# The recurrence of a hybrid decoder trunk: the inverse as two chains of two head pairs, and the order of a tick written anew

## What is computed

```python
def step(S, inp):
    r_t, d_t, kk_t, a_t, k_t, v_t = inp
    sa = jnp.einsum('bhvk,bhk->bhv', S, -kk_t)
    S = S * d_t[:, :, None, :] + sa[..., None] * (kk_t * a_t)[:, :, None, :] + v_t[..., None] * k_t[:, :, None, :]
    return S, jnp.einsum('bhvk,bhk->bhv', S, r_t)
...
y = jnp.moveaxis(ys, 0, 1)
mean = jnp.mean(y, axis=-1, keepdims=True)
var = jnp.mean(jnp.square(y - mean), axis=-1, keepdims=True)
y = (y - mean) * lax.rsqrt(var + GN_EPS) * lp['lnx_w'].reshape(N_HEADS_RWKV, HEAD_DIM) + lp['lnx_b'].reshape(N_HEADS_RWKV, HEAD_DIM)
y = y + jnp.sum(r_h * k_h * lp['r_k'], axis=-1, keepdims=True) * v_h
y = y.reshape(B, T, D_RWKV) * g
```

## Time and profile before

| | us |
|---|---|
| median of 3 runs (lowest to highest) | 2150.49 (2148.86 to 2151.88) |
| the profiled execution's own time | 2147.41 |
| its span, first to last instruction | 2145.8 |
| TensorE busy in the span | 2037.6 (95%) |
| VectorE, ScalarE, GpSimd busy | 1200.0 (56%), 622.0 (29%), 163.4 (8%) |

### The profile page before, as it was taken

The page is one execution under the profiler, slowest core; times in us unless marked ns, Lnnn a source line. Parts: engine busy times, 40 slices in busy tenths (PEclk is TensorE's granted clock), DMA queues, the critical chain, the costliest instruction groups (busy, mean ns, idle before and its releaser), DMA issues.

```text
span 2145.8 us, 37700 instructions
## 1 busy us (share of the span) xinstructions
PE 2037.6 (95%) x15476; PEld 1131.8 (53%) x15476; DVE 1200.0 (56%) x2401; ACT 622.0 (29%) x1401; POOL 163.4 (8%) x280
## 2 busy tenths in 40 slices
PE   8999999888888898999988999999999999999999
PEld 6445656788776774444444444444444444444443
DVE  4375654477775448776565445545453636363625
ACT  5005552222322226766644122111111111102020
POOL 3000000222221002222112000000000000000000
PEclk9999999999998997999999999999999999999999
DMA  7001113101013711000054601111111111111102
GB/s 220 0 0 30 30 30 112 43 4 24 4 34 104 194 51 55 11 6 11 1 172 145 201 1 40 39 40 39 40 40 40 39 40 39 39 40 41 43 35 84
DMA packets 96906, 115.77 MB, mean 54 GB/s; under 512 B 32252, under 2 KB 68029, under 8 KB 96671
## 3 DMA queue, kind: packets, MB, share of 16 engines
q1 hardware_dynamic: 90718, 101.82, 15.0%
q10 hardware_dynamic: 4480, 7.34, 1.2%
q0 software_dynamic: 1536, 4.20, 0.6%
HBM read 104.75 MB, written 12.64 MB: 55 GB/s over the span
## 4 chain that ended last, share of the span: by engine, by line
PE 83%; DVE 10%; ACT 4%; issue 2%; DMA 1%; ACTq 0%; POOL 0%; POOLq 0%; DVEq 0%
PE psum L1416 77%; PE psum L1951 2%; PE psum L1835 1%; ACT arena L1286 1%; PE psum L2008 1%; ACT arena L1272 1%; DVE arena L2467 1%; DVE arena L2643 1%; DVE arena L2617 1%; DVE arena L2510 1%; DVE arena L2494 1%; PE psum L1753 0%; PE psum L1501 0%; DVE arena L2457 0%; DVE arena L2506 0%
## 5 line engine op out<-in xcount | busy, mean ns | idle before, releaser
L1416 PE MATMUL psum<-arena 64*64 64x64 f32 (+13 forms) x12520 | 1794.8, 345 | 69.0 <-ACT arena L1286 20.1
L1416 PEld LDWEIGHTS psum<-arena 64*64 64x64 f32 (+5 forms) x12520 | 910.8, 150 | 845.4 <-issue 664.0
L2800 DVE TENSOR_TENSOR arena<-arena,psum 128x512 f32<-128x512 f32 x51 | 35.1, 688 | 318.5 <-PE psum L1416 318.5
L1389 ACT ACTIVATE arena<-psum 128x512 f32<-128x512 f32 x51 | 30.3, 595 | 437.3 <-PE psum L1416 344.7
L1378 ACT ACTIVATE arena<-arena 128x512 f32<-128x512 f32 x64 | 40.2, 628 | 274.2 <-DVE arena L2814 168.0
L938 POOL TENSOR_TENSOR arena<-arena,m_lev 128x256 f32<-128x256 f32 x82 | 59.7, 729 | 552.0 <-DVE arena L2448 362.7
L1272 ACT ACTIVATE arena<-psum 128x512 f32<-128x512 f32 (+1 forms) x148 | 80.7, 596 | 68.9 <-PE psum L1951 60.2
L2617 DVE TENSOR_REDUCE arena<-psum 128x1 f32<-128x640 f32 (+7 forms) x128 | 84.6, 703 | 14.8 <-PE psum L1416 13.2
L1286 ACT ACTIVATE arena<-psum,arena 128x640 f32<-128x640 f32 (+7 forms) x128 | 89.0, 704 | 10.7 <-DVE arena L2617 10.6
L1951 PEld LDWEIGHTS psum<-ident,arena 128*128 128x128 f32 x528 | 58.0, 143 | 46.1 <-issue 22.9
L2467 DVE TENSOR_TENSOR arena<-arena,psum 128x512 f32<-128x512 f32 x65 | 44.5, 684 | 62.8 <-PE psum L1416 62.8
(11 more groups left out here) (324 smaller groups left out, 1808.6 us busy)
## 6 DMA issues: line engine op xcount, KB each, us to landing
arena<-in_w_up_dram SPq DMA_DIRECT2D x7, 2048.0 KB, 7.6
arena<-in_w_down_dram SPq DMA_DIRECT2D x7, 2048.0 KB, 7.7
arena<-in_cache_slc_kv_dram SPq DMA_DIRECT2D x96, 128.0 KB, 2.7
arena<-in_cache_cmp_kv_dram SPq DMA_DIRECT2D x72, 128.0 KB, 3.3
arena<-in_x_prompt_dram SPq DMA_DIRECT2D x16, 512.0 KB, 12.8
arena<-in_cache_cmp_kv_dram ACTq DMA_DIRECT2D x56, 128.0 KB, 3.4
arena<-in_w_in_dram SPq DMA_DIRECT2D x13, 512.0 KB, 3.8
arena<-in_w_in_dram SPq DMA_DIRECT2D x2, 2048.0 KB, 19.6
```

The costliest lines, as they stand in the source:

```text
L1416: return nc.tensor.matmul(out, lhsT, rhs, start=start, stop=stop)
L2800: tt(u2, t_sb, bank_of(6), ALU.add).then_inc(sem("u_sum"), 1)
```

## The change

The inverse of a chunk becomes two chains, one for head pairs 0 and 1 and one for 2 and 3. Each has X, T and U in banks of its own, its copies and subtractions are half as wide, and its steps have semaphore counts of their own. The slots are gone: each engine's tick is one written list, and what isn't the chain stands between the chain's steps. Further: adding the identity (128x512) and the bonus rows (two operations of 128x256) go from VectorE to GpSimd; -u goes from VectorE to ScalarE; the centring takes one operation instead of two; the values are turned between the products of w; the weight (lnw) moves a tick later, to stand before the group norm's end; so does the reciprocal root on ScalarE; the products of the two masks are split (atrb early in bank 0, gtrk at the end in bank 7). The core of the diff (rests of the same kind left out):

```diff
-        inv_step = psum[:, 3 * 512 + 256:4 * 512 + 256]
-        inv_u, inv_t, inv_x = inv_step[:, 0:256], inv_step[:, 256:512], banks[4][:, 256:512]
+        inv_step = [psum[:, 512 * b + 384:512 * b + 640] for b in (3, 1)]
+        inv_u, inv_t = [v[:, 0:P] for v in inv_step], [v[:, P:2 * P] for v in inv_step]
+        inv_x = [banks[b][:, 256:384] for b in (4, 2)]
...
+            def bonus_rows(c):
+                if c == 0:
+                    pool.wait_ge(*once("bonus_out"))
+                else:
+                    pool.wait_ge(sem("rw_yo"), c)
+                link(nc.gpsimd.tensor_tensor(bv, vtok_r[c % 3], spread(bonus[:, c, :], 2, HD), ALU.mult))
+                nc.gpsimd.tensor_tensor(bv, bv, lnb, ALU.add).then_inc(sem("rw_bv"), 1)
...
             for c in range(NCH + 1):
+                pool.wait_ge(sem("rw_ab_sb"), 2 * c + 2)
+                turned = tu_r[c % 3].rearrange("p a b c d -> p (a b c) d")
+                nc.gpsimd.tensor_tensor(turned, turned, spread(eye2, 1, 2 * HP), ALU.add).then_inc(sem("rw_ti"), 1)
                 pool.wait_ge(sem("rw_prod_sb"), 2 * c + 1)
...
+                for i in range(min(nlev(c), 4)):
+                    level_mask(c, i)
+                if c >= 1:
+                    pool.wait_ge(sem("rw_vgsb"), c)
+                    bonus_rows(c - 1)
+                if nlev(c) == 5:
+                    level_mask(c, 4)
...
+            def l_act(c, i, half):
+                if i < nlev(c):
+                    act.wait_ge(sem("rw_x"), 2 * (lev0(c) + i) + half + 1)
+                    nc.scalar.activation(xsb[:, 2 * half:2 * half + 2], shaped(inv_x[half], 2, CH),
+                                         ACT.Copy).then_inc(sem("rw_xsb"), 1)
...
+            def value_turned(c, hp):
+                if hp == 0:
+                    if c == 0:
+                        pe.wait_ge(sem("f_mx"), UNITS)
+                    else:
                         pe.wait_ge(sem("rw_prod_sb"), 2 * c)
...
+            def w_ready(c):
+                if c == NCH:
+                    pe.wait_ge(*once("rw_pssb"))
+                    pe.wait_ge(sem("rw_st_yc"), 2 * NCH)
+                elif c > 0:
+                    pe.wait_ge(sem("rw_st_yc"), 2 * c)
```

VectorE's new tick (the guards of the edges left out):

```diff
+                for i in range(5):
+                    if i == 2 and new:
+                        ab_dve(n)
+                    if i == 2 and n - 2 == NCH:
+                        nub_dve()
+                    if i == 4 and outer:
+                        state_dve(n - 2)
+                        mean_dve(n - 2)
+                    if chain:
+                        l_dve(n - 1, i, 0)
+                        l_dve(n - 1, i, 1)
+                    if i == 0 and older:
+                        scale_dve(n - 3)
+                        o_dve(n - 3)
+                    if i == 1 and new:
+                        ar_dve(n)
+                    if i == 4 and new:
+                        gk_dve(n)
+                    if i == 4 and outer:
+                        var_dve(n - 2)
```

More of the change, by code:

```diff
@@ L1170, in s0_act, with o_act @@
+            def o_act(c):
+                act.wait_ge(sem("rw_yt"), c + 1)
+                if c == 1:
+                    act.wait_ge(sem("shift_stored"), 64)
+                src = shaped(banks[7][0:64, :], HP, 2, CH)
+                for h in range(2):
+                    ins = nc.scalar.activation(mixed[HALVES[h], HP:, CH * c:CH * c + CH], src[:, :, h, :], ACT.Copy)
+                ins.then_inc(sem("rw_mixed"), 1)
+            def s0_act(n, i):
                 b = n - 9
-                if k == 7 and 0 <= b < DEC_B:
+                if i == 1 and 0 <= b < DEC_B:
@@ L1178, in s0_act @@
+                if n == NCH + 2 and i == 4:
                     for b in range(DEC_B):
@@ new lines, in tu_product @@
+            def tu_product(c, i, half):
+                if i >= nlev(c):
+                    return
+                tu, n = tu_r[c % 3], lev0(c) + i
+                pe.wait_ge(sem("rw_xsb"), 2 * n + half + 1)
+                if n > 0 and i == 0:
+                    pe.wait_ge(sem("rw_t"), 2 * n + half - 1)
+                for hp in hps(half):
+                    for h, other in CROSSED:
+                        if i < nlev(c) - 1:
+                            mm(at_hp(inv_t[half][h], hp), tu[other, half, 0, hp % 2, :], xsb[other, hp, :])
+                        ins = mm(at_hp(inv_u[half][other], hp), xsb[other, hp, :], tu[other, half, 0, hp % 2, :])
+                ins.then_inc(sem("rw_tx"), 1)
@@ new lines, in outputs_turned @@
+            def outputs_turned(c):
+                pe.wait_ge(sem("rw_yo"), c + 1)
+                if c + 3 <= NCH:
+                    pe.wait_ge(sem("rw_vgsb"), c + 4)
+                if c > 0:
+                    pe.wait_ge(sem("rw_mixed"), c)
+                if c == NCH:
+                    pe.wait_ge(*once("rw_pstate_rows"))
+                for hp in range(HP):
+                    ins = nc.tensor.transpose(banks[7][0:64, hp * P:(hp + 1) * P], yc[:, hp, :], ident)
+                ins.then_inc(sem("rw_yt"), 1)
@@ new lines, in l_dve, with nub_dve, state_dve @@
+                    tt(flat, flat, inv_u[half], ALU.subtract).then_inc(sem("rw_t"), 1)
+            def nub_dve():
+                dve.wait_ge(sem("rw_nu"), NCH + 1)
+                for hp in range(HP):
+                    rowm = spread(row_of, 2, HD)
+                    ins = tt(nub[:, hp], spread(nu[:, hp, :], 1, DEC_B), rowm, ALU.mult)
+                ins.then_inc(once("rw_nub")[0], 1)
+            def state_dve(c):
+                dve.wait_ge(sem("rw_y"), c + 1)
+                if c == NCH:
+                    for hp, q in enumerate(SBANK):
+                        link(tt(sst[:, hp], sst[:, hp], shaped(banks[q], DEC_B, HD), ALU.add))
+                        end = dec_end[:, hp, NCH:]
+                        ins = tt(sst[:, hp], sst[:, hp], spread(end, 2, HD), ALU.mult)
+                    ins.then_inc(sem("rw_st_yc"), 1)
+                else:
+                    link(tt(st, st, shaped(banks[6][:, 0:256], HP, HD), ALU.add))
+                    tt(st, st, spread(dec_end[:, :, c], 2, HD), ALU.mult).then_inc(sem("rw_st_yc"), 1)
@@ new lines, in scale_dve, with o_dve @@
+            def scale_dve(c):
+                link(tt(yc, yc, lnw, ALU.mult))
+            def o_dve(c):
+                dve.wait_ge(sem("rw_yrs"), c + 1)
+                link(tt(yc, yc, spread(ystat[:, 1, :], 2, HD), ALU.mult))
+                dve.wait_ge(sem("rw_bv"), c + 1)
+                link(tt(yc, yc, bv, ALU.add))
+                tt(yc, yc, gtok_r[c % 3], ALU.mult).then_inc(sem("rw_yo"), 1)
+            for n in range(PERIODS):
+                new, chain, outer, older = n <= NCH, 0 <= n - 1 <= NCH, 0 <= n - 2 <= NCH, 0 <= n - 3 <= NCH
+                for i in range(5):
+                    if i == 2 and new:
[5 more added lines that the diff above has]
+                        mean_dve(n - 2)
+                    if chain:
+                        l_dve(n - 1, i, 0)
+                        l_dve(n - 1, i, 1)
+                    if i == 0 and older:
+                        scale_dve(n - 3)
[6 more added lines that the diff above has]
+                        var_dve(n - 2)
```

670 lines of the change are left out of this document (333 added, 337 removed).

## The result

The changed kernel takes 2132.86 us, the median of 4 executions (2127.86 to 2133.89), beside 2150.2 us for the kernel before, executed with it: a ratio of 0.9914 (95% interval 0.9897 to 0.9932). That is 17.3 us less where 25 were forecast. The range held it. The period of a tick didn't come out as forecast, and most of what follows is about that.

What follows compares the result with a forecast made beforehand. It took TensorE's work, plus the inverse's steps waiting for each other, as the bound. Ticks -26 us, tick 0 -1.9, tail +2.3 gave -25.6, taken as 25: median 2150.49 becomes 2125.5 us, range 2111 to 2143.

Steps and rivals of the forecast that it cites:

- the period: Length of one of ticks 1 to 16: 13.8 us forecast against 15.43 before, 26 us less in all.
- the odd 0.2 us I keep: Per tick: the difference between a clean tick of 15.2 us and the mean of 15.43, kept in the forecast.
- (b): Rival: VectorE and GpSimd, contending over SBUF, take most of the gain back; tick 14.7 us, 2141 us, chance 0.15.
- (c): Rival: a new wait, of the values behind the mask of gk, makes it slower; about 2159 us, chance 0.04.
- Work, 12.9 us a tick: TensorE's work in a tick before the change, summed from prices per record: 13.2 us, corrected to 12.9.
- Values packed, 0.46 us: Values' 16 records, between those of w on the other two quarters, save 0.46 us a tick.
- Waits for the chain and the mask, 0.2 + 0.25 + 0.4 us a tick: TensorE's remaining waits: X of level 1 0.2 us, level 2 0.25, values behind the mask of gk 0.4.
- The sample states' transposes, 0.3 us a tick: Four transposes in ticks 9 to 16 lose their cover: 0.6 us each such tick, 0.3 averaged over 16.
- Tick 0, -1.9 us: First tick: X of level 0 starts at about 388.8 instead of 390.74, 1.9 us less.
- Tail, +2.3 us: After the ticks: w of the sample chunk +1.5 us, later root +2.0, vanished wait for line 2519 -1.2.
- (a): Rival: work alone remains and stands fall in covered places; tick 12.9 to 13.2 us, 2113 us, chance 0.2.
- (d): Rival: small semaphore-bound steps cost more than the slots; 15.2 us a tick, 2148 us, chance 0.06.

Runs made afterwards that it cites:

- e5: Changed kernel with 16 products fewer a tick and narrower products (64 columns for ar and gk, 32 for y): 2117.53 us, ratio 0.9860.
- e8: Changed kernel with the values turned after all products of w instead of between them: 2133.83 us, ratio 0.9919.
- e3: Changed kernel again on another chip (48 empty instructions a tick were meant to be added, but the program that ran holds none): 2129.35 us, ratio 0.9896.
- e6: Kernel before, in its old order, with 16 products fewer a tick (y and gk, twice the columns): 2142.87 us, ratio 0.9972.
- e1: Changed kernel with 16 products fewer a tick, for y and gk, each with twice the columns: 2112.43 us, ratio 0.9820.
- e2: Changed kernel with the same number of products but half the columns in ar, gk and y: 2127.42 us, ratio 0.9901.
- v2: Changed kernel without product B (as v1), and with the identity added by VectorE again: 2125.42 us, ratio 0.9882.
- v1: Changed kernel without product B (8 a tick), VectorE taking T from ar's bank in two operations: 2126.04 us, ratio 0.9893.

## Why the prediction was right in sign and high in gain

**The step that failed** is the period: "13.3 + 0.2 + 0.3 = 13.8, against 15.43: 16 x 1.6 = 26 us less". It came out at 14.73 and 14.52 us in two profiled executions, 16 x 0.73 = 11.7 and 16 x 0.94 = 15.0 us less. The sum had the array's work and the waits for other engines. It had no term for the supply of TensorE's instructions; all that stood for it was "the odd 0.2 us I keep". For the kernel before that was about right: nine unnamed waits of the matmuls with 5.1 us, each at the end of a block, are 0.3 us a tick. In the changed kernel they are 24.3 us, 1.5 a tick. There were 59 blocks in both; before, TensorE was kept waiting by the chain and blocks came 4.19 us apart, and the change took that away.

The clue was hard to see. The large unnamed row that the prediction quotes, 31.5 us of weight loads in 63 waits, is mostly not supply, and to read it as steps of the inverse waiting for each other was half right: 15.7 us of it are the waits for the subtraction, and only 14 of the 63, with 7.2 us, come at the end of a block. The matmuls' row of nine waits is the one that points at it. The walk through a tick asked only which other engine would be late.

Rival (b) gave 14.7 us a tick, nearly the number measured, and by the prediction's own sign a period above 14.5 us meant (b) or (c). It was neither: matmuls wait 2.2 us in 16 ticks for VectorE and 0.8 for GpSimd, where (b) needs 0.9 us in each tick. A right number isn't a right reason. That the range held is in part luck too: it was wide because it took in (b).

**Term by term.**
- *Work, 12.9 us a tick.* Not refuted, and not tested by itself in the changed kernel: supply hides it. e5, with the least work, still takes 13.64. The unbroken row, 250 records in 6.86 us, is two blocks of instructions at 3.43 us; a block can come faster than 3.9 us, then, and what sets its time between is open.
- *Values packed, 0.46 us.* The packing is there; beside e8 it saves the array some 0.25 us a tick, and the tick nothing.
- *Waits for the chain and the mask, 0.2 + 0.25 + 0.4 us a tick.* The matmuls' named waits together are 3.2 us, 0.2 a tick; with the weight loads' (3.7, 1.8 and 1.7 us, in part the same standings) they are at most 0.7 a tick. That for the mask of gk (line 2595) came in only 3 ticks of 16. They can't be read singly, since a TensorE that stands for its supply arrives late at every wait.
- *Sizes.* 277 ns for the copy of 128x128 (estimate 0.28) and 418 ns for the subtraction of 128x256 (0.41) were right. Line 2655, the middle one of the three operations that end the group norm, meets GpSimd and takes nearly twice its time; lines 2653 and 2656 around it keep their 0.42 us (mean ns behind the busy us):

```profile
L2612 DVE TENSOR_TENSOR arena<-arena,psum 128x256 f32<-128x256 f32 x128 | 48.8, 418 | 70.4 <-PE psum L1452 70.4
L2655 DVE TENSOR_TENSOR arena<-arena 128x256 f32<-128x256 f32 x14 | 11.2, 801 | 0.5
...
L2656 DVE TENSOR_TENSOR arena<-arena 128x256 f32<-128x256 f32 x14 | 6.0, 426 | 0.5
L2653 DVE TENSOR_TENSOR arena<-arena 128x256 f32<-128x256 f32 x14 | 5.9, 425 | 0.5
```

In the tick shown line 2655 runs from 506.26 to 507.11 under a mask that ends at 506.83, 0.28 us earlier, the very figure of the earlier trace rows; GpSimd's mask took its usual 0.72 us. VectorE stood as forecast, one operation in a tick, and it costs nothing, as VectorE is busy 9.4 of 14.7 us. But "no GpSimd operation stretched", true of the kernel before (its masks take 722 to 734 ns), isn't true of the changed one: eight of its 82 masks take 0.93 to 0.99 us. Each of the eight started 0.02 to 0.08 us after the decay product (line 2634), which kept its 0.42 us:

```profile
440.77 0.42 DVE L2634 TENSOR_TENSOR arena<-arena,dec_end 128x256 f32<-128x256 f32 x1
...
440.79 0.99 POOL L952 TENSOR_TENSOR arena<-arena,m_lev 128x256 f32<-128x256 f32 x1 [2.23 <-PE psum L1452]
```

So whichever of the two starts first keeps its time and the other stands, as in the rule that the prediction quotes and sets aside. Masks late by up to 0.26 us did no harm that shows: matmuls wait 0.8 us for a mask in 16 ticks, once.
- *The sample states' transposes, 0.3 us a tick.* The four records at 504.76 take 0.46 us, with the next work at 505.15; ticks 4 to 8, before they begin, have a period of 15.0 us, no shorter than the mean. Nothing of them can be seen under the supply.
- *Tick 0, -1.9 us.* X of level 0 was forecast for about 388.8, behind GpSimd's mask, and the first row below has it. (The copy of the keys in tick 0 came 1.7 us earlier, 3.0 in e3; in e6, which has the old order, it came 1.3 us earlier, so the starts of stages differ by a microsecond between chips.)
- *Tail, +2.3 us.* w of the sample chunk stood 1.81 us (0.69 before; +1.5 was forecast, +1.1 came). The row names no releaser, but the centring that w now waits for (line 2641) ends at 639.53, 0.1 us before, and no instruction packet starts between 631.73 and 640.64. And the 2.43 us for line 2519 in tick 17 are gone, as forecast. The last outputs wait 2.55 us for line 2656, and line 1964 (1820 before) starts at 667.18, 13.9 us earlier, not 23; 13.4 of these are there at the last copy of the keys. From that copy to the end of the span the two kernels differ by 0.1 us (2145.8 - 637.1 and 2132.3 - 623.7). The copy stands nearer to the end of a tick than it did, so this doesn't exclude a tail that is one or two microseconds longer.

```profile
388.80 0.51 PE L1452 MATMUL psum<-arena 64*64 64x64 f32 x10 [0.76 <-POOL arena L952]
```

```profile
627.94 0.62 PE L1818 MATMUL psum<-ident,arena 128*64 128x128 f32 x4
...
639.63 0.33 PE L1452 MATMUL psum<-ident,arena 64*64 64x64 f32 x4 [1.81 <-issue]
...
666.71 0.63 PE L1818 MATMUL psum<-ident,arena 128*64 128x128 f32 x4 [2.55 <-DVE arena L2656]
667.18 1.91 PE L1964 MATMUL psum<-ident,arena 128*128 128x128 f32 x16
```

**The sum.** In the profiled executions 2147.41 - 2133.89 = 13.5 us: 11.7 in the 16 ticks, 1.7 before them, 0.1 after. The medians differ by 17.3, and e3's profiled execution by 18.0 with 15.0 in the ticks. Of the forecast's 26 us in the ticks, 11 to 14 didn't come; by e1, e2 and e5 the supply of instructions held them back.

**The rivals.** (a), work alone, 12.9 to 13.2 us a tick: not what happened, and whether the array could do it no run shows, as supply stands in front of it. (b) is refuted by the matmuls' short waits for VectorE and GpSimd, with v2 beside v1, (c) by line 2595's small row. (d), small steps that eat the slots' gain at 15.2 us a tick, is refuted by e1, which has the same semaphores and waits and takes 13.68.

## What to carry to other kernels

When a stage of many short products on TensorE gets denser, count its instructions, not only its columns: here a tick couldn't be shorter than its instructions / 256 x some 3.9 us, 15 ns an instruction, and a float32 product is four of them. Look for standings of the matmuls before "issue" at equal counts of records (here 126), with a packet of the instruction queue before each. Where they are there, wider products and fewer of them are worth more than fewer columns, better packing or a shorter chain. And split an unnamed row before using it: here half of the weight loads' row was a named wait of the matmuls seen twice, and the small row of the matmuls, nine waits, was the term that grew fivefold once the named waits were gone.

## What was not expected of the hardware

- TensorE's supply of instructions was slower than its array. In nine kernels with enough to do, blocks of 256 came 3.90 to 3.99 us apart on average over the stage. The packet itself is short (two in 8 us take 1.4% of 16 engines' time, 0.9 us each, and 1.2 us on the mean of the 59); TensorE resumes 2.3 to 2.95 us after its start. Single blocks came 3.42 to 4.78 us apart in the changed kernel. Why the next packet isn't asked for earlier no run here shows.
- The queue of the array mixes products on different quarters over a longer stretch than they were written in: values written after w ran at 20 ns a record, interleaved ones at 18.
- Empty instructions written for TensorE are not in the program that runs, so they can't be used to test its supply.
- VectorE, with both inputs in SBUF, stood until 0.28 us after GpSimd's operation had ended (801 ns on the mean of line 2655 instead of about 420), where GpSimd started first. Where VectorE started first, GpSimd's mask took 0.93 to 0.99 us instead of 0.73 and VectorE's operation its usual 0.42.
